# Last stage of a hybrid encoder layer: residual added on GpSimd, norm row in PSUM, four tiles combined without TensorE

## What is computed

```python
def rms_norm(x, g):
    y = xf * lax.rsqrt(jnp.mean(xf * xf, axis=-1, keepdims=True) + NORM_EPS)
    return (y * g.astype(jnp.float32)).astype(x.dtype)
...
    # routed_experts: two expert rows per token, weighted by wts
    return jnp.einsum('tkd,tk->td', y_assign.reshape(T, TOPK_IN_GROUP, D), wts.astype(yb.dtype))
...
    x = x + g2 * hierarchical_moe(h, ...)
    return rms_norm(x, norm_final), ...
```

## Time and profile before

| what | us |
|---|---|
| median of three executions | 1714.07 |
| lowest, highest | 1712.88, 1718.18 |
| span of the profiled execution | 1713.1 |
| first load of the last stage issued | 1659.77 |
| VectorE's first instruction of the last stage | 1665.81 |
| VectorE's last instruction ends | 1707.92 |
| last output issued | 1707.95 |

### The profile page before, as it was taken

How to read it: one execution, slowest core, us unless ns; L and a number is a source line. 1 busy time by engine, 2 the same in 40 slices (tenths; PEclk the granted TensorE clock), 3 DMA queues, 4 the chain that set the end, 5 groups by cost and what they waited for, 6 DMA issues and landing times. The chain is left out here.

```text
span 1713.1 us, 26036 instructions
## 1 busy us (share of the span) xinstructions
PE 1612.2 (94%) x10744; PEld 1408.8 (82%) x10744; DVE 1258.1 (73%) x1496; ACT 926.1 (54%) x1102; POOL 307.9 (18%) x203
## 2 busy tenths in 40 slices
PE   5999999999899999998998995999999999999956
PEld 4899889988898989997997883788888888888842
DVE  5743774377677686865656457899999999999937
ACT  5633244325436353453203123788898888889822
POOL 2410010001101010012000001122334433232230
PEclk9999999999999999999999996999999999999977
DMA  9121013101216233243346326899999999999955
GB/s 334 40 76 39 14 38 118 40 14 38 94 51 190 77 113 105 84 138 127 120 152 213 138 105 263 309 372 389 382 386 392 390 384 381 385 381 398 373 211 224
DMA packets 129552, 345.98 MB, mean 202 GB/s; under 512 B 16369, under 2 KB 72281, under 8 KB 103769
## 3 DMA queue, kind: packets, MB, share of 16 engines
q1 hardware_dynamic: 113704, 312.42, 50.6%
q0 software_dynamic: 9824, 17.88, 2.8%
q10 hardware_dynamic: 5904, 13.99, 2.2%
HBM read 316.16 MB, written 43.81 MB: 210 GB/s over the span
## 5 line engine op out<-in xcount | busy, mean ns | idle before, releaser
L148 PE MATMUL wo_psum_m<-h_hi,x_w_hi 128*128 128x364 f32 (+1 forms) x1184 | 403.6, 341 | 4.6 <-ACT x_x L1030 1.5
L149 PE MATMUL wo_psum_m<-h_lo,x_w_hi 128*128 128x364 f32 (+1 forms) x1184 | 390.3, 330 | 0.0
L150 PE MATMUL wo_psum_m<-h_hi,x_w_lo 128*128 128x364 f32 (+1 forms) x1184 | 390.2, 330 | 0.0
L148 PEld LDWEIGHTS wo_psum_m<-h_hi,x_w_hi 128*128 128x128 f32 x1184 | 223.8, 189 | 17.1 <-issue 7.2
L149 PEld LDWEIGHTS wo_psum_m<-h_lo,x_w_hi 128*128 128x128 f32 x1184 | 223.9, 189 | 2.5
L150 PEld LDWEIGHTS wo_psum_m<-h_hi,x_w_lo 128*128 128x128 f32 x1184 | 223.8, 189 | 0.0
L729 POOL CAST x_w_hi<-x_w 128x1024 fp32r<-128x1024 f32 x44 | 78.3, 1780 | 648.3 <-PE wo_psum_m L150 628.0
L2307 POOL DMA_INDIRECT scratch_y<-e_y,all_tbl x32 | 74.2, 2319 | 374.0 <-ACT e_y L2431 374.0
L1459 DVE TENSOR_TENSOR x_w_lo<-x_w,x_w_hi 128x1024 fp32r<-128x1024 f32 x52 | 64.5, 1241 | 91.0 <-POOL x_w_hi L729 61.8
L1434 DVE TENSOR_REDUCE x_sc<-x_diag 64x64 f32<-64x448 f32 x119 | 110.9, 932 | 1.0
L148 PE MATMUL e_psum_y<-e_d_hi,e_hid_hi 128*128 128x512 f32 x256 | 103.6, 405 | 5.3 <-DVE e_d_lo L2520 5.3
(11 more groups left out here) (389 smaller groups left out, 3647.9 us busy)
## 6 DMA issues: line engine op xcount, KB each, us to landing
mg_ring_hi<-in_w_e_gate SPq DMA_DIRECT2D x34, 1024.0 KB, 10.1
mg_ring_lo<-in_w_e_down SPq DMA_DIRECT2D x34, 1024.0 KB, 8.5
mg_ring_hi<-in_w_e_up SPq DMA_DIRECT2D x32, 1024.0 KB, 8.6
mg_ring_lo<-in_w_e_up SPq DMA_DIRECT2D x32, 1024.0 KB, 8.8
mg_ring_lo<-in_w_e_gate SPq DMA_DIRECT2D x30, 1024.0 KB, 9.9
mg_ring_hi<-in_w_e_down SPq DMA_DIRECT2D x30, 1024.0 KB, 8.7
x_w<-in_w_in SPq DMA_DIRECT2D x44, 512.0 KB, 3.9
scratch_gate<-x_x ACTq DMA_DIRECT2D x16, 544.0 KB, 3.1
```

What stands on the lines that cost most here:

```text
L148: nc.tensor.matmul(out, lhs[0], rhs[0], start=start, stop=False)
L149: nc.tensor.matmul(out, lhs[0], rhs[1], start=False, stop=False)
L150: return nc.tensor.matmul(out, lhs[1], rhs[0], start=False, stop=stop)
```

## The change

Four things are changed in the last stage, and nothing ahead of it but two names and the number of diagonals:

1. The residual of tiles 0 to 7 is added by GpSimd. The ninth tile's stays on VectorE.
2. ScalarE copies the row `nf` into PSUM once, into the two banks of the experts' gate and up products, and VectorE's last multiplication reads it there.
3. Tiles 0, 1, 4 and 7 are combined without TensorE, in place of 0 and 1. GpSimd makes diagonals for five tiles in place of seven.
4. The tiles are worked on in the order 0, 1, 4, 2, 3, 7, 5, 6, 8 (`TURN`), in the same groups of 3, 3, 2 and 1 by place. They are loaded in the old order and written out in the new. VectorE does six tiles ahead of `normed(0)` where it did four.

```diff
-        p_g, p_u, p_h = s.psum("g", [P, F]), s.psum("u", [P, F]), s.psum("h", [P, KF, N])
+        p_gu, p_h = s.psum("gu", [P, 2, F]), s.psum("h", [P, KF, N])
+        p_g, p_u, p_nf = p_gu[:, 0, :], p_gu[:, 1, :], p_gu[:, :, :].rearrange("p a f -> p (a f)")
...
         GROUPS = [(0, 3), (3, 6), (6, 8), (8, NTT)]
+        TURN = [0, 1, 4, 2, 3, 7, 5, 6, 8]
+        ALONE = [0, 1, 4, 7]
+        SUMMED = [t for t in TURN if t not in ALONE]
...
-        ALONE = 2
...
# SyncE
-            for t in range(NTT):
+            for i, t in enumerate(TURN):
                 t0, n = TILES[t]
                 dst = outs[0][0, t0:t0 + n, :] if t < NT else outs[1][0]
-                sp.wait_ge(out_ready, t + 1)
+                sp.wait_ge(out_ready, i + 1)
                 sp.dma_start(dst, ys[0:n, t, 0, :]).then_inc(out_done, 16)
...
# GpSimd
-                    for t in range(ALONE, NTT):
+                    for t in SUMMED:
...
             pool.sem_inc(combined, 1)
+            pool.wait_ge(x2_in, 16 * 3)
+            for i, t in enumerate(TURN[:-1]):
+                pool.wait_ge(y_gated, i + 1)
+                nc.gpsimd.tensor_tensor(x3[t], x3[t], ys[:, t, 1, :], ALU.add).then_inc(x3_ready, 1)
...
# ScalarE
+            act.wait_ge(hid_done, NE)
+            act.wait_ge(rows_in, 16 * 3)
+            nc.scalar.activation(p_nf, nf, ACT.Copy).then_inc(nf_kept, 1)
             scale_y(0)
             scale_y(1)
-            for t in range(NTT):
-                square(t)
...
+            square(0)
+            scale_y(4)
+            square(1)
+            square(2)
+            root(0)
+            scale_y(7)
+            for i in range(3, 6):
+                square(i)
+            root(1)
+            square(6)
+            square(7)
+            root(2)
+            square(8)
+            root(3)
...
# VectorE
-                dve.wait_ge(y_gated, t + 1)
-                V.tensor_tensor(x3[t][0:n], x3[t][0:n], yt, ALU.add).then_inc(x3_ready, 1)
+                if t == NT:
+                    dve.wait_ge(y_gated, NTT)
+                    V.tensor_tensor(x3[t][0:n], x3[t][0:n], yt, ALU.add).then_inc(last_ready, 1)
...
-                for t in range(ta, tb):
-                    V.scalar_tensor_tensor(out=ys[0:n, t, 0, :], in0=x3[t][0:n], scalar=stat[0:n, 5, t:t + 1], in1=nf[0:n],
+                for p in range(ta, tb):
+                    t = TURN[p]
+                    V.scalar_tensor_tensor(out=ys[0:n, t, 0, :], in0=x3[t][0:n], scalar=stat[0:n, 5, p:p + 1], in1=p_nf[0:n],
                                            op0=ALU.mult, op1=ALU.mult).then_inc(out_ready, 1)
...
+            dve.wait_ge(nf_kept, 1)
+            for i in range(6):
+                mixed(i)
+            normed(0)
+            mixed(6)
+            mixed(7)
+            normed(1)
+            mixed(8)
+            normed(2)
+            normed(3)
...
# TensorE
-            for t in range(ALONE, NTT):
+            for i, t in enumerate(SUMMED):
                 n = TILES[t][1]
                 pe.wait_ge(y_in[t], 16)
-                pe.wait_ge(diag_ready, t + 1 - ALONE)
-                if t >= ALONE + 2:
-                    pe.wait_ge(y_gated, t - 1)
+                pe.wait_ge(diag_ready, i + 1)
+                if i >= 2:
+                    pe.wait_ge(y_gated, TURN.index(SUMMED[i - 2]) + 1)
```

More of the change, by code:

```diff
@@ L2232, in experts @@
         y_rows = y_d.rearrange("(t k) d -> t k d", k=2)
-        xg_clear = s.sem("xg_clear")
+        xg_clear, nf_kept, last_ready = s.sem("xg_clear"), s.sem("nf_kept"), s.sem("last_ready")
         s.soft += router.sems
@@ L2466, in scale_y, with square @@
             def scale_y(t):
-                n = TILES[t][1]
[L2468 to L2475, removed]
+                n, i = TILES[t][1], ALONE.index(t)
+                act.wait_ge(y_in[t], 16)
+                if i >= 3:
+                    act.wait_ge(y_summed, i - 2)
+                nc.scalar.activation(y1[0:n, i % 3, :], ys[0:n, t, 0, :], ACT.Copy, scale=wts[0:n, t, 0:1]).then_inc(y_scaled, 1)
+            def square(i):
+                t = TURN[i]
+                n = TILES[t][1]
+                if t == NT:
+                    act.wait_ge(last_ready, 1)
+                else:
+                    act.wait_ge(x3_ready, i + 1)
+                if i:
+                    act.wait_ge(sumsq, i)
                 nc.scalar.activation(junk[0:n, :], x3[t][0:n], ACT.Square, scale=float(D) ** -0.5,
-                                     accum_out=stat[0:n, 0, t:t + 1]).then_inc(sumsq, 1)
+                                     accum_out=stat[0:n, 0, i:i + 1]).then_inc(sumsq, 1)
             def root(i):
                 ta, tb = GROUPS[i]
-                n = TILES[ta][1]
+                n = TILES[TURN[ta]][1]
                 act.wait_ge(sumsq, tb)
@@ L2614, in _, with mixed @@
                     V.tensor_tensor(v_act[:, :], v_act[:, :], p_u[:, :], ALU.mult).then_inc(v_hid_ready, 1)
-            def mixed(t):
+            def mixed(i):
+                t = TURN[i]
                 n, g = TILES[t][1], int(t == NT)
                 yt = ys[0:n, t, 1, :]
-                if t < ALONE:
-                    dve.wait_ge(y_scaled, t + 1)
-                    V.scalar_tensor_tensor(out=yt, in0=yt, scalar=wts[0:n, t, 1:2], in1=y1[0:n, t % 3, :],
+                if t in ALONE:
+                    a_ = ALONE.index(t)
+                    dve.wait_ge(y_scaled, a_ + 1)
+                    V.scalar_tensor_tensor(out=yt, in0=yt, scalar=wts[0:n, t, 1:2], in1=y1[0:n, a_ % 3, :],
                                            op0=ALU.mult, op1=ALU.add).then_inc(y_summed, 1)
-                    dve.wait_ge(y_summed, t + 1)
+                    dve.wait_ge(y_summed, a_ + 1)
                     V.tensor_tensor(yt, yt, g2[0:n, g, :], ALU.mult).then_inc(y_gated, 1)
                 else:
-                    dve.wait_ge(sum_done, t + 1 - ALONE)
-                    V.tensor_tensor(yt, sums[t % 2][0:n, :], g2[0:n, g, :], ALU.mult).then_inc(y_gated, 1)
-                dve.wait_ge(y_gated, t + 1)
-                V.tensor_tensor(x3[t][0:n], x3[t][0:n], yt, ALU.add).then_inc(x3_ready, 1)
+                    m = SUMMED.index(t)
+                    dve.wait_ge(sum_done, m + 1)
+                    V.tensor_tensor(yt, sums[m % 2][0:n, :], g2[0:n, g, :], ALU.mult).then_inc(y_gated, 1)
+                if t == NT:
+                    dve.wait_ge(y_gated, NTT)
+                    V.tensor_tensor(x3[t][0:n], x3[t][0:n], yt, ALU.add).then_inc(last_ready, 1)
             def normed(i):
                 ta, tb = GROUPS[i]
-                n = TILES[ta][1]
+                n = TILES[TURN[ta]][1]
                 q = [stat[0:n, j, ta:tb] for j in range(6)]
@@ L2744, in _ @@
                     m.then_inc(v_y_done, 1)
-            for t in range(ALONE, NTT):
+            for i, t in enumerate(SUMMED):
                 n = TILES[t][1]
                 pe.wait_ge(y_in[t], 16)
-                pe.wait_ge(diag_ready, t + 1 - ALONE)
-                if t >= ALONE + 2:
-                    pe.wait_ge(y_gated, t - 1)
+                pe.wait_ge(diag_ready, i + 1)
+                if i >= 2:
+                    pe.wait_ge(y_gated, TURN.index(SUMMED[i - 2]) + 1)
                 for c in (0, HALF):
                     for k in range(2):
-                        m = nc.tensor.matmul(sums[t % 2][0:n, c:c + HALF], diagonal(t)[0:n, k, 0:n], ys[0:n, t, k, c:c + HALF],
+                        m = nc.tensor.matmul(sums[i % 2][0:n, c:c + HALF], diagonal(t)[0:n, k, 0:n], ys[0:n, t, k, c:c + HALF],
                                              start=(k == 0), stop=(k == 1))
```

3 lines of the change are left out of this document (removed).

## The result

The changed kernel takes 1719.94 us (median of eight runs, 1717.11 to 1721.63), the kernel before 1714.91 us in the same measurement (eight runs, 1712.88 to 1718.18). The ratio on record is 1.0023, with a 95% interval from 1.0012 to 1.0033. That is 3.9 us slower, and the two medians alone are 5.0 us apart; either is within the 0.3%, 5.1 us, that the prediction called no change. The profiled execution of the changed kernel has a span of 1716.6 us, 3.5 us more than that of the kernel before.

A forecast was written before the change was run, and what follows sets the result against it. VectorE's last-stage instructions were taken to bound the kernel: -0.9 us from the schedule and +5.2 us of waits gave +4.3, a span of 1717.4 us, plus 1.0 to the median: 1718.4 us, range 1711.5 to 1723.

The forecast's parts named there:

- +4.3: Move of VectorE's last instruction: -0.9 us from the schedule, +5.2 us from refining steps waiting for GpSimd's adds.
- The 1.0 us from span to median: Added to the forecast span of 1717.4 us, as the runs' median stood above the profiled span: 1714.07 against 1713.1.
- The wait for tile 7: VectorE waits for tile 7's load, landed at 1684.8, and starts it at 1686.1 after ScalarE's scaling of 1.15 us.
- The price of an add: GpSimd's residual add of 128x1024 takes 2.1 us, between 1.04 and 3.6 us.
- The three waits: Refining steps on VectorE wait for GpSimd's adds: 2.1 us in the first group, 1.0 and 2.1 in the second.
- rows 6: Trace near 540 us: GpSimd's cast gets in through a 0.04 us gap between VectorE instructions with two SBUF inputs.
- Rival 1: VectorE's small refining steps don't wait for GpSimd's adds; 1713.2 us, or 1711.6 to 1714.6; chance 0.27 with rival 3.
- rival 2: GpSimd's add costs 2.6 us or more, so each of the three waits grows; 1720 to 1728 us; chance 0.14.
- rival 3: TensorE's sum of tile 8 is 3.1 us later after idleness, costing 1.4 us if small steps don't wait; within Rival 1's 0.27.

The follow-up runs named there:

- e1: The changed kernel with ScalarE writing each group's root into PSUM, so refining steps have one SBUF input; ratio 1.0013 to the kernel before.
- e7: e6 with the roots in SBUF again; ratio 1.0013 to the kernel before.
- e3: The changed kernel with VectorE reading the norm's row from SBUF, the copy to PSUM still made; ratio 1.0027 to the kernel before.
- e2: The changed kernel with the nine loads issued in the order of TURN, tile 7 sixth; ratio 1.0024 to the kernel before.
- e6: The changed kernel with roots in PSUM, order 0, 1, 3, 2, 4 to 8, only 0, 1, 3 without TensorE, norm groups of two; 1710.12 us, ratio 0.9965.

## Why the prediction held

**What bounds and what moves with it.** VectorE's end moved from 1707.92 to 1711.44, +3.5 us, and the span by the same 3.5; +4.3 was forecast. The time moved by 3.9 us by the ratio and 5.0 by the medians. The median itself, 1719.94, is 1.5 us above the 1718.4, and 0.8 of that is the starting point: 1714.07 was the median of three runs of the kernel before, and eight have 1714.91. The 1.0 us from span to median was of two different executions; each execution on record takes 1.7 to 2.1 us more than its own span.

**The wait for tile 7.** The load landed 21.0 us after its issue, at 1684.2, where the earlier trace rows had 21.5 and 1684.8, and VectorE began tile 7 at 1685.46, forecast 1686.1. These 0.6 us are most of the 0.8 by which +4.3 was too much. From there to the end the prediction had 20.9 us of work and 5.2 us of waits, together 26.1; measured 1711.44 - 1685.46 = 26.0. That the sums agree so well is partly luck, since it is 20.2 us of work and 5.8 of waits. The work is shorter because an instruction that doesn't depend on the one ahead begins some 0.1 us before that one's record ends (the first norms end at 1690.90 + 3.67 = 1694.57, the next gate begins at 1694.48). The waits are longer by the price of an add and by one that the forecast didn't have: GpSimd's third add ran until 1685.89, and the sum of tile 7 took 1.51 us in place of 1.28.

**The price of an add.** 2.1 us was taken from rows of casts and of one small add; alone it takes 2.34. The Trainium skill's figure (GPSIMD Engine Reference, section 3.1 Elementwise — side-by-side cycle accounting), 4497 ns for 2048 columns, gave an estimate of 2.3 us and was the better one.

**The three waits.** Forecast 2.1, 1.0 and 2.1; measured, beyond the work, 2.33 - 0.16 = 2.17, 1.40 - 0.15 = 1.25 and 2.28 - 0.16 = 2.12, in the places named: one in the first group, two in the second, none in the third. The choice between nothing and a whole add was the forecast's riskiest step, and rows 6 were the right ones to take it by. One reading of them is loose: a cast of 1.04 us that ended at 542.07 began at 541.03, 0.13 us before the recorded end of L1414 (539.88 + 1.28 = 541.16) and not in the gap behind it. The add at 1668.38 shows the same, 2.34 us before its end being 1669.28, 0.14 us before the recorded end of VectorE's sum. So the waiting instruction has some 0.14 us more than the gap that the records show. The Trainium skill's rule (SBUF — State Buffer, section Who interferes with whom) holds here down to an instruction of three columns (0.16 us of work took 2.33), which e1 and e7 show by taking the second SBUF input away and giving it back. Rival 1 fell with the first row of a long step, rival 2 with the 2.34 us.

**The slow sum.** The sum of tile 8, that of rival 3, took 7.06 us and was hidden by the second group's norm, as told. That it would surface when the waits go was put at 1.4 us; in e1 it was 1.95.

**The rest.** The copy to PSUM took 1.03 us in ScalarE's idle time, the norms didn't change, and fewer sums on TensorE gained nothing. In e3 the copy proved to be without use in this kernel, which the prediction hadn't said.

## What to carry to other kernels

Work moved from VectorE to GpSimd is only off VectorE if VectorE's instructions beside it have at most one input in SBUF, the tiniest included: look for short dependent steps, and put one operand of each into PSUM. Ask of each engine what it waits for next once a wait is gone; here a sum at TensorE's lower clock stood behind the one removed in e1, and TensorE's sums behind the late load in e2, and the gain came only when order, groups and operands fitted together (e6, 0.9965).
